# Seven sample batches' cached values spread as octets over eight head pairs, the eighth batch between the blocks of the output projection

## What is computed

```
def fox_attend(q, cq, qpos, k, ck, kpos, v):
    # softmax(q.k/sqrt(d) + cq[t] - ck[s]) over keys with kpos <= qpos
...
def fox_sample(h, ck_pool, cv_pool, cl_pool, page_table, w_in, b_f, w_out):
    q, k, v, z, logf = fox_project(h, w_in, b_f)
    kp = ck_pool[page_table].reshape(B, P, N_HEADS, HEAD_DIM)
    vp = cv_pool[page_table].reshape(B, P, N_HEADS, HEAD_DIM)
...
    o = fox_attend(q, c_new, qpos, k_all, c_all, kpos, v_all)
    y = (o * jax.nn.silu(z)).astype(h.dtype) @ w_out
```

## Time and profile before

| | us |
|---|---|
| median of 3 runs (1989.58 to 1993.14) | 1991.42 |
| the profiled execution's own time | 1999.29 |
| its span | 1997.6 |
| PE busy (92% of the span) | 1837.1 |
| DVE busy (56%) | 1124.7 |
| ACT busy (27%) | 547.3 |
| POOL busy (15%) | 296.4 |
| PE span of the attend stage, from scores(0, 0) to the last sample_last | 1353.4 to 1886.5 |
| output projection, from then to the last block's matmul | 1886.5 to 1975.3 |

### The profile page before, as it was taken

One profiled execution on the slowest core, in us unless ns is written; L12 is line 12 of the kernel. 1 busy time (PEld: TensorE's weight loads), 2 busy tenths in 40 slices (PEclk: granted clock), 3 DMA queues, 4 the chain that ended last, 5 costly groups with the idle time before them and its releaser, 6 DMA issues.

```text
span 1997.6 us, 37941 instructions
## 1 busy us (share of the span) xinstructions
PE 1837.1 (92%) x15120; PEld 1362.1 (68%) x15120; DVE 1124.7 (56%) x1810; ACT 547.3 (27%) x1241; POOL 296.4 (15%) x328
## 2 busy tenths in 40 slices
PE   4999999999999989899989999885999998999997
PEld 3877887787788767677778777773545554555676
DVE  5434544474465367877776777663545554554533
ACT  5121121121111143111112111212444444454521
POOL 0000000000000003444444444330000000000100
PEclk9999999999999989899999999996899999999999
DMA  5111111111112156899999999989999899999721
GB/s 139 38 45 53 43 45 42 48 43 49 43 48 64 32 177 231 286 339 313 319 319 351 321 323 308 329 296 333 336 330 305 301 333 327 311 327 344 271 85 56
DMA packets 228677, 414.49 MB, mean 207 GB/s; under 512 B 17553, under 2 KB 137010, under 8 KB 228238
## 3 DMA queue, kind: packets, MB, share of 16 engines
q1 hardware_dynamic: 168364, 252.17, 38.0%
q0 software_dynamic: 42160, 150.54, 21.2%
q10 hardware_dynamic: 17986, 9.42, 1.7%
HBM read 370.85 MB, written 41.94 MB: 207 GB/s over the span
## 4 chain that ended last, share of the span: by engine, by line
PE 52%; DMA 22%; DVE 13%; SPq 5%; issue 4%; POOL 2%; ACT 2%; POOLq 0%; DVEq 0%; ACTq 0%
DMA k_raw<-in_cache_k_dram,k_idx 16%; PE ps_a L812 5%; PE ps_a L814 4%; PE ps_a L813 4%; DVE kt L1293 4%; PE ps_b L812 3%; PE ps_b L814 3%; PE ps_b L813 3%; PE ps_c L812 3%; DMA d_sb<-decay 3%; PE ps_b L1592 3%; PE ps_c L814 3%; PE ps_c L813 3%; SPq L359 3%; PE ps_b L1560 2%
## 5 line engine op out<-in xcount | busy, mean ns | idle before, releaser
L1293 DVE STREAM_TRANSPOSE kt<-k_raw 128x1024 f32<-128x1024 f32 x256 | 309.9, 1232 | 145.7 <-DMA k_raw<-in_cache_k_dram,k_idx 140.6
L353 POOL DMA_INDIRECT k_raw<-in_cache_k_dram,k_idx x256 | 256.3, 1001 | 449.2 <-DVE kt L1293 291.0
L812 PE MATMUL ps_a<-h_hi,w_hi 128*128 128x512 f32 x656 | 263.2, 401 | 3.2 <-DVE w_lo L1115 3.2
L814 PE MATMUL ps_a<-h_hi,w_lo 128*128 128x512 f32 x656 | 256.4, 391 | 0.0
L813 PE MATMUL ps_a<-h_lo,w_hi 128*128 128x512 f32 x656 | 256.4, 391 | 0.0
L1115 DVE TENSOR_TENSOR w_lo<-w_raw,w_hi 128x1024 fp32r<-128x1024 f32 x97 | 109.1, 1125 | 163.1 <-ACT w_hi L642 160.4
L1592 PE MATMUL ps_b<-v_pg,pt_s 128*16 128x256 f32 x2048 | 147.4, 400 | 17.2 <-DMA v_pg<-in_cache_v_dram 16.1
L812 PE MATMUL ps_b<-h_hi,w_hi 128*128 128x512 f32 x384 | 154.2, 401 | 2.7 <-DVE w_lo L1115 2.7
L812 PEld LDWEIGHTS ps_a<-h_hi,w_hi 128*128 128x128 f32 x656 | 123.5, 188 | 39.1 <-issue 10.8
L814 PE MATMUL ps_b<-h_hi,w_lo 128*128 128x512 f32 x384 | 150.0, 391 | 0.0
L813 PE MATMUL ps_b<-h_lo,w_hi 128*128 128x512 f32 x384 | 149.7, 390 | 0.0
(11 more groups left out here) (284 smaller groups left out, 2854.5 us busy)
## 6 DMA issues: line engine op xcount, KB each, us to landing
v_pg<-in_cache_v_dram SPq DMA_DIRECT2D x256, 512.0 KB, 7.6
w_raw<-in_w_in_pool_dram SPq DMA_DIRECT2D x32, 512.0 KB
w_raw<-in_w_in_attn_dram SPq DMA_DIRECT2D x32, 512.0 KB
w_raw<-in_w_out_pool_dram SPq DMA_DIRECT2D x16, 512.0 KB
s_scr<-ss_st ACTq DMA_DIRECT2D x64, 128.0 KB, 6.2
s_in<-s_scr SPq DMA_DIRECT2D x16, 512.0 KB, 7.4
d_sb<-decay SPq DMA_DIRECT2D x32, 256.0 KB, 8.5
z_scr<-x_st SPq DMA_DIRECT2D x8, 528.0 KB, 5.0
```

The source lines that it names most:

```text
L353: pool.indirect_dma_start(k_raw[:, k, :], None, cache_rows, bass.IndirectOffsetOnAxis(ap=k_idx[:, u, k:k + 1], axis=0)).then_inc(k_full[k] ...
L812: nc.tensor.matmul(ps, ah, bh, start=j == 0, stop=False)
L814: mm = nc.tensor.matmul(ps, al, bh, start=False, stop=j == last)
L1293: V.transpose(kt[u % 2][:, :, 32 * k:32 * k + 32], k_raw[:, k, :].rearrange("p (i c) -> p i c", c=32)).then_inc(dve_kt, 1)
```

## The change

The 32 pairs of slots of the stage are counted as g = 4·pair + slot // 2. Those with g = 0, 8, 16 and 24 (slots 0 and 1 of pairs 0, 2, 4 and 6) get no sample work. The other 28 hold the 28 octets of batches 0 to 6 in order, so that a batch no longer starts with its pair. The share of the pages between the two slots of an octet stays as it was (`V_SPLIT`). The octets of batch NT = 7 stand in the output projection: octet 0 before block 0, octets 1, 2 and 3 after blocks 0, 1 and 2, `sample_last` after block 2. The steps that prepare a batch move along with its octets: `new_scores`, `common_max` and `sample_out` now come in the slot in which the batch before ends (`opened`), and in pair 0 the preparation of batch 0 comes behind slot 0's prompt work and in slot 1. `sample_out(7)` and the sample rows' projection come one or two blocks later. Seven of the eight weight splits now stand after pair 7. On SP the weights' loads are spread over the pages of pair 7, and the loads of pair q+1 are tied to the first page used in pair q (`FIRST_PAGE`).

```diff
-        wo_at = [big_at(n) for n in (9024, 10048, 0, 1024, 4160, 5184, 6208, 7232)]
+        wo_at = [big_at(n) for n in (9024, 10048, 0, 1024, AT_F + 4096, 5184, 6208, 7232)]
...
+        NT = NB - 1
+        octets = iter((b_, o_) for b_ in range(NT) for o_ in range(4))
+        OCTET = {g_: next(octets) for g_ in range(4 * NB) if g_ % 8}
+        FIRST_PAGE = [8 * sum(g_ < 4 * p_ for g_ in OCTET) for p_ in range(NB)]
+        V_SPLIT = (2, 2, 3, 4)
...
+        def opened(p, s):
+            if s % 2 == 0:
+                return None
+            oc = octet(p, s)
+            return 0 if (p, s) == (0, 1) else oc[0] + 1 if oc and oc[1] == 3 else None
...
@@ sync_attend
+                if q == NB - 1 and n in (0, 10, 13, 16):
+                    w_out_rows(4 + (0, 10, 13, 16).index(n))
+                if q == NB - 1 and n == 22:
+                    sp.wait_ge(pe_s, 16 * (NB - 1))
+                    w_out_rows(0)
+                if q == NB - 1 and n in (25, 28, 31):
+                    w_out_rows((n - 22) // 3)
...
+            for n in range(VR, NB * PAGES):
+                v_page(n // PAGES + 1, n % PAGES)
+                for q in range(NB):
+                    next_pair(q, n - FIRST_PAGE[q])
+                next_batch(n // PAGES, n % PAGES)
...
@@ tensor_attend, pair
-                    if s == 0:
-                        sample_turn(b, 0)
-                    if s == 7 and b < NB - 1:
-                        new_scores(b + 1)
+                    now, after, fresh = octet(b, s), next_octet(b, s), opened(b, s)
+                    if s % 2 == 0 and now and now[1] == 0:
+                        sample_turn(*now)
+                    if fresh is not None:
+                        new_scores(fresh, b, s)
...
@@ tensor_attend, output projection
                 if i == 0:
                     prompt_values(NB - 1, SLOTS - 1)
+                    sample_turn(NT, 0)
+                    octet_pages(NT, 0, 0, 8)
+                if i < 3:
+                    sample_turn(NT, i + 1)
+                if i == 2:
+                    new_turn(NT)
...
                 mm.then_inc(pe_y, 1)
+                if i < 3:
+                    octet_pages(NT, i + 1, 0, 8)
                 if i == 2:
+                    sample_last(NT)
+                if i == 4:
...
@@ scalar_attend
-            sample_exp(0, 0)
             for b in range(NB):
                 pair(b)
-            act.wait_ge(pe_t2, len(T2) * NB)
+            act.wait_ge(dve_s, NT * N_S + 4)
+            high_w(5)
+            sample_exp(NT, 0)
+            high_w(6)
+            high_w(7)
+            sample_evac(NT, 0)
+            sample_exp(NT, 1)
+            act.wait_ge(pe_t2, T2_PROMPT)
             high_w(0)
...
@@ vector_attend, pair
+                    if fresh == 0:
+                        sample_scores(0, 2)
+                        sample_scores(0, 3)
+                    if fresh is not None:
+                        new_scores(fresh)
                     prompt_norm(b, s, 0)
                     prompt_norm(b, s, 1)
-                    at = (0, 2, 4, 6) if b else (2, 4, 5, 6)
-                    if s in at and more:
-                        sample_scores(b + 1, at.index(s))
+                    if (b, s) == (0, 0):
+                        sample_scores(0, 0)
+                        sample_scores(0, 1)
+                    if s % 2 == 0 and now:
+                        sample_scores(now[0] + 1, now[1])
...
-            for n in range(4, KT8):
+            for n in range(1, KT8):
                 low_w(n)
```

More of the change, by code:

```diff
@@ new lines, in build @@
+        T2 = []
+        for p_ in range(NB):
+            for s_ in range(SLOTS):
+                oc_, nx_ = octet(p_, s_), next_octet(p_, s_)
+                if s_ % 2 == 0 and oc_ and oc_[1] == 0:
+                    T2.append(("s",) + oc_)
+                T2 += [(p_, h_, s_, f_) for h_ in range(2) for f_ in range(len(fills(s_, h_)))]
+                if nx_ and nx_[1]:
+                    T2.append(("s",) + nx_)
+                    if nx_[1] == 3:
+                        T2.append(("n", nx_[0]))
@@ L1385, in t2_free, with t2_at @@
[L1385 to L1388 removed]
+        def t2_at(key):
+            return T2.index(key)
+        def t2_free(key):
+            same = [j for j in range(T2.index(key)) if t2_name(T2[j]) == t2_name(key)]
             return same[-1] + 1 if same else 0
         y_ps = ((ps_a[:, 0:512], ps_a[:, 512:DM]), (ps_c[:, 512:DM], b7[:, :]))
[L1392 removed]
@@ L1577, in new_turn, with sample_pages, octet_pages @@
                 pe.wait_ge(act_e, b * N_E + N_E)
-                pe.wait_ge(act_t2, t2_free(b, ("n",)))
+                pe.wait_ge(act_t2, t2_free(("n", b)))
+                if b == NT:
+                    pe.wait_ge(dve_op, NB * SLOTS)
                 for hh in range(2):
-                    mm = nc.tensor.transpose(b6[0:TS, P * hh:P * hh + P], s_sb[:, hh, PAST // 4:SW], ident)
+                    mm = nc.tensor.transpose(t2_bank(("n", b))[0:TS, P * hh:P * hh + P], s_sb[:, hh, PAST // 4:SW], ident)
                 mm.then_inc(pe_t2, 1)
-            def sample_pages(b, s, first, last):
-                pe.wait_ge(act_t2, t2_at(b, ("s", s // 2)) + 1)
-                for p in range(V_FIRST[s] + first, V_FIRST[s] + min(last, V_FIRST[s + 1] - V_FIRST[s])):
+            def sample_pages(q, s, first, last):
+                if octet(q, s) is None:
+                    return
+                b, o = octet(q, s)
+                half = V_SPLIT[s // 2]
+                start, n = (half, 8 - half) if s % 2 else (0, half)
+                if first < n:
+                    octet_pages(b, o, start + first, start + min(last, n))
+            def octet_pages(b, o, first, end):
+                pe.wait_ge(act_t2, t2_at(("s", b, o)) + 1)
+                for p in range(8 * o + first, 8 * o + end):
                     if p == 0:
@@ L1628, in pair @@
                     sample_pages(b, s, 4 if s else 0, PAGES)
-                    if s == SLOTS - 1:
-                        sample_last(b)
-                    if s in (1, 3, 5):
-                        sample_turn(b, (s + 1) // 2)
+                    if fresh:
+                        sample_last(fresh - 1)
+                    if after and after[1]:
+                        sample_turn(*after)
                     if s < SLOTS - 1:
@@ L1636, in pair @@
                         scores(b + 1, 0)
-                    if s == 5:
-                        new_turn(b)
+                    if after and after[1] == 3:
+                        new_turn(after[0])
             pe.sem_inc(pe_pv, VR)
@@ L1675, in tensor_attend @@
                     mm.then_inc(pe_sm, 1)
[L1676 removed]
+                if i == 5:
                     pe.wait_ge(dve_sm, 1)
@@ L1902, in pair @@
             def pair(b):
-                more = b < NB - 1
                 for s in range(SLOTS):
+                    now, fresh = octet(b, s), opened(b, s)
                     prompt_max(b, s, 0)
```

176 lines of the change are left out of this document (82 added, 94 removed).

## The result

The changed kernel takes **2020.64 us** (median, 2017.79 to 2022.02), the kernel before 1992.28 us beside it: ratio 1.0141, interval 1.0122 to 1.0159. It is slower by 28 us, where 12 us less were forecast. The range (1961 to 1997) doesn't hold it.

What follows compares the result with a forecast made beforehand. Prediction: PE and DMA look nearly full, but pairs 1 to 6 lose 38.3 us, mainly to d_sb's latency, not average bandwidth. Terms 23.5 - 16 - 19.3 = -11.8 us gave 1979.6 us from 1991.42, range 1961 to 1997.

Steps and rivals of the forecast that it cites:

- The projection, +23.5: Output projection: 19.4 us of added PE work, plus waits in the passage from pair 7 and for pages; +23.5 us.
- 2.6 taken: Passage from pair 7 to block 0: PE waits 2.6 us while ACT does splits, exponentials and the copy.
- 1.5 taken: Projection: pages of octets 1 to 3 land while a block runs; 1.5 us for the first, bounds 0 and 6.
- The start and pair 0, -16: Ahead of and in pair 0: PE no longer waits for batch 0; -16 us, bounds -20 and -8.
- Pairs 1 to 7, -19.3: Pairs 1 to 7 together: 422.2 us against 441.5, so -19.3 us.
- Base 57.6 us: Each of pairs 1 to 7: what PE needs when nothing is late, read from pair 7; 403.2 us in all.
- Freed slots, new order, clock: -3 + 2 + 6 = +5: Pairs 1 to 7: emptied slots save 3 us, the new-score step ahead of scaling costs 2, the clock in slot 1 6.
- Late data: 14 us: Batches 1, 4, 5 and 6: waits for d_sb, taken as latency, 3.5 us each; 14 us, bounds 5 and 44.7.
- It isn't a lack of bandwidth on average: Pairs 1 to 6: DMA share 0.57 in a pair's first slots, over 1 in the middle; 6.4 us lost each.
- The end: End of the kernel: the same chain as before, so no change.
- The first: Rival 1, slower: d_sb and DVE's kept order keep the 6.4 us loss per pair; +18.9 us, about 2010, chance 0.20.
- three signs of being wrong: d_sb waits staying at 4.5 us each, late pages of octets 1 to 3 in the projection, empty slots shrinking by the full octet.

Runs made afterwards that it cites:

- a_cols: The changed kernel with half the columns of every value page left out of the load from the ninth page on: 1980.32 us, pairs 1 to 7 419.3 us.
- c_cols: A variant with 31 octets unbroken from pair 0's second place, the last in the projection, with half of each value page's columns not loaded: 1964.96 us.
- b_early: The kernel before, with the second half of d_sb's score rows issued behind the batch's second page after the octet's turn instead of its twelfth: 1996.57 us, ratio 1.0058.

## Why the prediction was wrong, point by point

The profiled sum was -11.8 us, measured +18.5.

- **The projection, +23.5:** right within 2 us, +25.4. PE waited 1.71 us for pt_s (2.6 taken) and 2.9 us for two pages of octet 1 (1.5 taken); behind these the clock fell (0.72 from 1903 to 1909), some 1.4 us that had no term.
- **The start and pair 0, -16:** right, -14.65 and +0.8 ahead of it. Slot 2 begins at 1387.16 (1386 forecast), pair 0 ends at 1431.2 (1429). The wait came where it was put, 10.9 us long instead of some 14:

```profile
1382.18 1.97 PE L1577 MATMUL b<-con,p_p 128*128 128x128 f32 x8 [10.88 <-DVE p_p L1873]
```

- **Pairs 1 to 7, -19.3:** wrong, +7.0; these 26.3 us are nearly the whole miss. Three steps of it:
  - *Base 57.6 us.* Right: 57.94 with no data late.
  - *Freed slots, new order, clock: -3 + 2 + 6 = +5.* Measured in `a_cols`: +14.0. Freed slots 0 and 1 -2.6 (-3 taken) and slot 2 behind them, with its fallen clock, +6.1 (+6 taken) came out. Mis-sized was the batch's end and beginning inside a pair: 0.6 us in five pairs were taken, +2 in all; measured are 1.7 us a pair in `c_cols` and 2.5 in slots 3 and 4 of pair 2, and all that is left of the 14 is 10.5. That the whole of it is the batch's end and beginning is argued, not shown.
  - *Late data: 14 us.* Measured 29.2. This is the step that failed, in its mechanism: it put the loss down to the latency of d_sb, pair by pair, and took waits for pages to "nearly vanish" (under 3 us); measured were 7.3 us of waits for d_sb and 13.1 for pages. "It isn't a lack of bandwidth on average" was true and not to the point. The average held two things apart that the eight buffers can't join: time in which DMA has nothing to do, and time in which it is full and moves little (233 GB/s at a share of 1.05). That the share would fall and the buffers be full after each pause came out (0.72 to 0.74 in those pairs), but eight pages last 16 us (32 are used in some 64), and DMA had been full again for 60 us when the page was late. What fills it around that page is named above: the next pair's rows, q and k more than v_pr. The wait for d_sb was a symptom of the same queue; `b_early` cured it and not the pair.
- **The end:** held for unchanged, and so it is, 11.3 us behind the last matmul in both.
- **The rivals.** The first had the sign and almost the size (+18.9, measured +18.5 in the trace and 28.4 by the medians), but not the cause: it wanted d_sb's waits to stay at 4.5 us each, and they fell to 7.3 in all. That its size fits is luck. Of the three signs of being wrong that the prediction named, only late pages in the projection came, and those cost 2.9 us; late pages in the pairs, which decided it, weren't among them. On the clock the Trainium skill, page "TensorE: Matmul & The Clock Gate", section "HAM oscillation — how this bites in real kernels", says that bursts shorter than the waits between them are throttled each time. In the kernel before, pair 2 is such a case: bursts of 0.6 us between waits of 0.8 to 1.6, and a clock of 0.61 behind them. Slot 1 of the changed kernel's pair 2 isn't: its matmuls run for 3.5 us between waits of 2.0 and 1.9, and the clock falls all the same (0.79, 0.78, 0.86).

That the time went up by 28.4 us and not 18.5 is not explained.

## What to carry over

Before work is taken from a stage whose DMA share is high, run it with half the bytes of each row (half the rows relieved nothing here): one run says what late data cost and what doesn't come back. A transfer stream with a fixed number of buffers can't use an empty place longer than its buffers, so thinning one place in eight gave less here than moving the whole row by one, which keeps each period the same. And where a cyclic order is shifted against another, every phase is a different kernel: try all of them (59.6, 61.6 to 67.7, 65.5 to 72.8 us a pair here) before choosing.
